# A two-layer decoder step: order of the key groups in layer 1, gate pages by GpSimd, index keys by pairs, outputs turned whole

## The chip, the core and the metric

The kernel runs on one core of a Trainium2 chip. Times are microseconds of that core. TensorE (PE) multiplies and turns tiles and loads its weights on a unit of its own (PEld); VectorE (DVE), ScalarE (ACT) and GpSimd (POOL) work elementwise; SyncE (SP) and, here and there, ScalarE and GpSimd issue the DMA transfers. A transpose is work of PE: it takes the tile and an identity matrix and writes to PSUM, from where another engine copies it.

## What is computed

One inference step of a decoder with two layers: 256 prompt tokens and 8 sample sequences with one new token each behind 2048 cached ones, in float32. Layer 0 is sparse attention with an indexer, layer 1 attention with cumulative forget gates. In each layer four more heads attend to 256 memory tokens, and a mixture of 16 experts follows. The cached keys, values, index keys and gates lie in pages of 128 tokens, found through a page table.

```python
ki_past = pool_ki[page_table].reshape(Bd, P, IDX_DIM)           # layer 0: index keys, 64 wide
sc = indexer_scores(qi, wi, ki_all); _, sel = lax.top_k(sc, 256)
...
k_all = concat([pool_k[page_table], k_new])                     # layer 1: 2048 + 1 keys, 4 heads of 128
lf_all = concat([pool_lf[page_table], logf_new])
c = cumsum(lf_all)                                              # 12 gates for each token
s = q @ k.T * HEAD_DIM ** -0.5 + c_q - c_k
o = softmax(s) @ v
...
mem: o = softmax(qm @ mk.T) @ mv                                # 4 heads, 256 tokens
h = layer_norm(alpha * h + concat([o, o_mem]) @ w_o)
h = layer_norm(alpha * h + hier_moe(h))
```

## The kernel before

**Tiles.** X holds the 264 tokens (256 + 8) turned, as 16 chunks of 128x264. Weights, cached keys and cached values come in units of 2 MB (128x4096) through a ring of six places; `plan` fixes the order of the units and, by its last argument, the place at which some of them must lie. SP issues them in that order and waits for each place to be free. A `slab` is 64 matmuls that multiply two units with X (or with the memory tokens, tile AT) into four PSUM banks, and ScalarE's `slab` copies the four banks out (`slab_copied` counts). Work can be set beside a slab: the function given as `beside` is called with x = 0 to 15 after every fourth matmul.

**Layer 0's index.** `turn_cached` turns the cached index keys (64 wide) for pairs of sequences: for each of four pages and both sequences one matmul with the identity puts 64 rows of the bank. Each is two records in the trace. Eight such steps stand between slab work and the products of the indexer. When the last score is there VectorE selects the top 256 out of 2049 (`MAX8`, line 2112).

**Layer 1's order on PE.** The `else` branch of the program below: the slabs q0, q1, kv1 (values), q2, kv0 (keys), then four times `key_products` (line 982, two sequences each: scores of the new token against 2 x 2048 keys), with the slabs qm, mkv0 (memory keys) and mkv1 (memory values) between them. Before each group VectorE must have turned the four units of keys (line 2209) in their ring places. Gate pages come on SP's queue, 128 of 6 KB (`GATES_AFTER`); VectorE puts them in place (line 2192), `gates_turned` turns their 16 tiles beside slab kv0, and ScalarE copies them. Rows of keys and memory (`late_rows`, `natural`, line 765) are turned in the middle of group 3. `sample_scores` then turns the cached memory keys (16 steps, line 1034) and multiplies (line 1019), and turns the scores (line 1046).

**Attention.** A loop of n = 0 to 21 alternates the prompt's heads (lines 1064 to 1096) with the values of one sequence (line 1114, two units each in layer 1). ScalarE copies the outputs of a sequence (`ov_copy`), and `fold` multiplies them with a constant that picks the rows of its heads; each fold is 2 (layer 0) or 4 matmuls (layer 1, line 1157), and 4 for a pair of sequences in memory (line 1162). In the end ScalarE copies the folded outputs into AT and counts `at_done`, on which the router's weights and the output projection (line 1251) wait.

**Layer norm.** At a layer's end VectorE centres and scales X in quarters of 4 chunks (lines 2384, 2387), ScalarE applies the parameters (line 1881), and the first slab of the next layer follows. `idle_products` (line 1271) are matmuls without use of their result.

## Time and profile before

| | us |
|---|---|
| median of 3 runs | 2137.57 |
| lowest, highest | 2133.9, 2138.18 |
| the profiled execution's own time | 2131.57 |
| its span in the trace | 2129.8 |
| PE busy in the span | 2047.3 |
| VectorE busy | 773.1 |
| ScalarE busy | 387.6 |
| GpSimd busy | 25.6 |

The mean granted clock of PE is 0.989 of full speed. Layer 0's projections and index end near 330 us, its attention at 432, its experts at 1060; layer 1's projections begin at 1071, its attention ends at 1476, and its experts run to the end. A view in order of time has the start of a group of like instructions, the time until its last one ends, the line, result and sources, and how many records there are; idle time before it and what ended it stand in brackets. In a fence, three dots mark rows left out.

### The profile page before, as it was taken

Reading aid. Unit: us, or ns where it says so; the run is one execution under the profiler, and the core shown is the slowest. Engines: PE = TensorE matmul, PEld = TensorE weight load, DVE = VectorE, ACT = ScalarE, POOL = GpSimd, SP = SyncE. Lnnn points to the kernel's source line nnn. Section 1 sums busy time; section 2 is a strip of 40 time slices with the busy share of each in tenths; the row PEclk is TensorE's granted clock in tenths of the full one; section 3 lists DMA queues with packets and bytes.
Section 4 is the critical chain, followed back from the end, with each engine's and each line's share of the span. In section 5 each row is a group of like instructions: output and inputs, shape, how many; then the busy total and the mean of one; then the engine's idle time right before and its main releaser. Section 6 shows DMA issues by size and latency. Waiting matters only on the chain.

```text
span 2129.8 us, 33851 instructions
## 1 busy us (share of the span) xinstructions
PE 2047.3 (96%) x13356; PEld 1291.9 (61%) x13356; DVE 773.1 (36%) x1278; ACT 387.6 (18%) x932; POOL 25.6 (1%) x43
## 2 busy tenths in 40 slices
PE   8999998999999999999989999899999999999998
PEld 7778886888744435353478867566886344343434
DVE  0229998601752221212330433441138312122223
ACT  1220103500421101010221100342024111010122
POOL 0000002100000000000000000000000000000000
PEclk9999999999999999999999999999999999999999
DMA  9834579964279999999944778899631999999994
GB/s 283 247 119 150 177 252 295 312 235 157 80 292 426 422 429 418 428 426 426 392 139 125 285 277 297 319 386 382 232 132 57 423 426 418 427 414 425 418 427 181
DMA packets 210787, 647.43 MB, mean 304 GB/s; under 512 B 55400, under 2 KB 84857, under 8 KB 181089
## 3 DMA queue, kind: packets, MB, share of 16 engines
q1 hardware_dynamic: 194497, 633.99, 77.2%
q10 hardware_dynamic: 14624, 7.48, 1.4%
q0 software_dynamic: 1536, 4.20, 0.6%
q8 instruction: 87, 1.43, 0.3%
q14 instruction: 43, 0.35, 0.1%
HBM read 639.62 MB, written 5.96 MB: 303 GB/s over the span
## 4 chain that ended last, share of the span: by engine, by line
PE 78%; DMA 11%; SPq 6%; issue 2%; DVE 2%; ACT 1%; ACTq 0%; DVEq 0%
PE bank L749 19%; PE bank L1452 15%; PE bank L1251 11%; PE bank L1499 9%; PE bank L1513 6%; DMA ring<-in_w_down 5%; SPq L427 4%; DMA ring<-in_w_up 4%; PE bank L1425 4%; PE bank L982 3%; DMA ring<-in_cache_b_k 1%; PE bank L1335 1%; PE bank L869 1%; SPq L424 1%; PE bank L1222 1%
## 5 line engine op out<-in xcount | busy, mean ns | idle before, releaser
L1452 PE MATMUL bank<-ring,AT 128*64 128x512 f32 x2048 | 457.5, 596 | 12.2 <-DMA ring<-in_w_up 9.0
L749 PE MATMUL bank<-X,ring 128*128 128x264 f32 x1664 | 387.3, 390 | 6.2 <-ACT X L1881 6.2
L749 PEld LDWEIGHTS bank<-X,ring 128*128 128x128 f32 x1664 | 313.1, 191 | 65.0 <-issue 13.3
L1452 PEld LDWEIGHTS bank<-ring,AT 128*64 128x64 f32 x2048 | 144.0, 137 | 286.3 <-issue 278.8
L1625 ACT ACTIVATE arena<-bank 128x512 f32<-128x512 f32 (+9 forms) x307 | 135.5, 479 | 735.2 <-PE bank L749 252.3
L1499 PE MATMUL bank<-ring,arena 128*64 128x512 f32 x1024 | 224.4, 594 | 18.7 <-ACT arena L1625 13.8
L2601 DVE TENSOR_TENSOR X<-bank,X 128x264 f32<-128x264 f32 x256 | 110.7, 432 | 361.8 <-PE bank L1513 359.8
L1251 PE MATMUL bank<-AT,ring 128*128 128x264 f32 x1024 | 232.3, 390 | 0.0
L1251 PEld LDWEIGHTS bank<-AT,ring 128*128 128x128 f32 x1024 | 196.6, 192 | 34.0
L1499 PEld LDWEIGHTS bank<-ring,arena 128*64 128x64 f32 x1024 | 73.2, 137 | 159.5 <-issue 147.6
L2209 DVE STREAM_TRANSPOSE ring<-ring 128x4096 f32<-128x4096 f32 x24 | 106.5, 4442 | 100.8 <-DMA ring<-in_cache_b_k 100.6
L1625 ACT ACTIVATE AT<-bank 128x512 f32<-128x512 f32 (+4 forms) x180 | 84.0, 493 | 321.9 <-PE bank L1425 193.4
L1513 PE MATMUL bank<-arena 128*128 128x264 f32 x512 | 138.8, 402 | 0.0
L1513 PEld LDWEIGHTS bank<-arena 128*128 128x128 f32 x512 | 89.0, 189 | 70.0 <-DVE X L2601 46.7
L749 PE MATMUL bank<-AT,ring 128*128 128x256 f32 x512 | 111.6, 380 | 0.0
L749 PEld LDWEIGHTS bank<-AT,ring 128*128 128x128 f32 x512 | 97.0, 190 | 14.8 <-issue 1.7
L2112 DVE MAX8 arena<-arena 8x8 f32<-8x2049 f32 (+1 forms) x48 | 79.6, 1659 | 42.7 <-ACT arena L1625 41.3
L1425 PE MATMUL bank<-arena 128*128 128x256 bf16 x768 | 89.5, 273 | 0.0
L1425 PEld LDWEIGHTS bank<-arena 128*128 128x128 bf16 x768 | 74.3, 98 | 13.8 <-issue 2.1
L2113 DVE MATCH_REPLACE8 arena<-arena 8x2049 f32<-8x2049 f32 (+1 forms) x48 | 79.1, 1647 | 0.0
L982 PE MATMUL bank<-ring,arena 32*32 32x512 f32 x1536 | 57.9, 641 | 11.0 <-DVE ring L2209 9.7
L2614 DVE TENSOR_TENSOR arena<-bank,arena 128x512 f32<-128x512 f32 x16 | 11.1, 691 | 150.7 <-PE bank L1452 150.7
(361 smaller groups left out, 1344.8 us busy)
## 6 DMA issues: line engine op xcount, KB each, us to landing
ring<-in_w_gate SPq DMA_DIRECT2D x64, 2048.0 KB, 15.3
ring<-in_w_up SPq DMA_DIRECT2D x48, 2048.0 KB, 16.1
ring<-in_w_down SPq DMA_DIRECT2D x48, 2048.0 KB, 13.2
ring<-in_w_o SPq DMA_DIRECT2D x16, 2048.0 KB, 15.7
ring<-in_w_up SPq DMA_DIRECT2D x32, 1024.0 KB, 7.8
ring<-in_w_down SPq DMA_DIRECT2D x32, 1024.0 KB, 16.0
ring<-in_cache_b_k SPq DMA_DIRECT2D x128, 256.0 KB, 5.5
ring<-in_cache_b_v SPq DMA_DIRECT2D x128, 256.0 KB, 8.1
```

Source lines behind the costliest of these rows:

```text
L427: eng.dma_start(dst(g + k), cache[bass.ds(page, 1)].rearrange("a p w -> (a p) w")).then_inc(sem, 16)
L749: mm = pe.matmul(B[at + f][:, 0:n_tok], u[:, c * 512 + f * P:c * 512 + (f + 1) * P], src[8 * half + c][:, 0:n_tok], start=(half == 0 and c ...
L982: mm = pe.matmul(B[bank + r][out, :], a.Qz[kv // 2][rows, q:q + 32], tiles[b][rows, :, kv * P + 32 * d:kv * P + 32 * d + 32], start=(b < 2 ...
L1251: mm = pe.matmul(B[bank0 + f][:, 0:T], u[:, c * 512 + f * P:c * 512 + (f + 1) * P], Ac[8 * half + c], start=(half == 0 and c == 0), stop=( ...
L1425: mm = pe.matmul(B[GATHER_BANKS[q]][:, c * 2 * P:(c + 1) * 2 * P], M.part[t][k][:, at:at + P], M.sel[:, t * 2 * P:(t + 1) * 2 * P], start= ...
L1452: mm = pe.matmul(B[bank][64 * s:64 * s + 64, :], M.xsT[:, at:at + 64], ring[slots[s][0]][:, c * FE:(c + 1) * FE], start=(half == 0 and c = ...
L1499: mm = pe.matmul(B[2 + q][64 * s:64 * s + 64, :], M.hT[:, at:at + 64], ring[slots[s][0]][:, j * D + q * 512:j * D + (q + 1) * 512], start= ...
L1513: pe.matmul(B[2 + c % 4][:, 0:T], M.ys[:, c * P:(c + 1) * P], M.gt[a], start=True, stop=True).then_inc(sm("scattered"), 1)
L1625: return act.activation(out, in_, ACT.Copy, scale=scale)
L2112: link(dve.max(m8, sc))
L2209: dve.transpose(t[:, :], t[:, :]).then_inc(S("keys_made"), 1)
L2601: dve.tensor_tensor(Xc[c], B[2 + c % 4][:, 0:T], Xc[c], ALU.add).then_inc(sm("scatter_added"), 1)
```

## The change

- Index keys of two sequences lie side by side (`index_key`), and one transpose turns a page of both.
- `fold` becomes `turn_out`: the whole output tile is turned, and VectorE's `place_out` adds up the rows that belong together, in the loop from n = 4 on and behind it. `new_values` moves to the second prompt item and gets columns of its own, which VectorE adds at the end; ScalarE's last copies go. `turn_out(x)` waits until x outputs have been placed.
- Layer 1's slabs and key groups stand in another order; the second memory slab comes behind the last key group, the score turns lie beside it, the exp in front of its copies; memory rows are turned behind it and kept in another place. The bank set of the key groups is now 0 in both layers, and ring places follow the order of use.
- GpSimd issues the gate pages, after its memsets.
- The first quarter of the layer norm is scaled by chunks, and five idle products follow the layer norm of layer 0 on PE.

Names below: `consts` holds the identity, `ring` the 2 MB units, `bank` PSUM. PE of layer 1 from the slab in front of key group 1 to the group itself, before (key products are L982, L1003 after; slabs L749, L747 after):

```order
L749 MATMUL bank<-X,ring 128x264 [waits full5_l1,slab_copied]
L749 MATMUL bank<-X,ring 128x264 x31
L749 MATMUL bank<-X,ring 128x264 [waits full2_l1]
L749 MATMUL bank<-X,ring 128x264 x31
L982 MATMUL bank<-ring,arena 32x512 [waits keys_made]
L982 MATMUL bank<-ring,arena 32x512 x127
L992 MATMUL bank<-consts 32x32 [waits natural_copied,slab_copied]
L992 MATMUL bank<-consts 32x32
```

And after:

```order
L747 MATMUL bank<-X,ring 128x264 [waits full5_l1,slab_copied]
L747 MATMUL bank<-X,ring 128x264 x31
L747 MATMUL bank<-X,ring 128x264 [waits full0_l1]
L747 MATMUL bank<-X,ring 128x264 x31
L787 MATMUL bank<-consts,arena 128x128 [waits lf_ready,slab_copied]
L787 MATMUL bank<-consts,arena 128x128 x15
L1003 MATMUL bank<-ring,arena 32x512 [waits keys_made]
L1003 MATMUL bank<-ring,arena 32x512 x127
L1017 MATMUL bank<-consts 32x32 [waits lf_copied,natural_copied,slab_copied]
L1017 MATMUL bank<-consts 32x32
```

Behind the same slab length stand now the 16 gate transposes (L787), and the group waits for the gates' copies only at its end.

PE from the turned rows in the middle of key group 3 (`late_rows`) on, before:

```order
L765 MATMUL bank<-consts,AT 128x128 [waits natural_copied]
L765 MATMUL bank<-consts,AT 128x128 x3
L765 MATMUL bank<-consts,AT 128x128 [waits natural_copied]
L765 MATMUL bank<-consts,AT 128x128 x3
L982 MATMUL bank<-ring,arena 32x512 x64
L992 MATMUL bank<-consts 32x32 [waits natural_copied,slab_copied]
L992 MATMUL bank<-consts 32x32
L1009 MATMUL bank<-consts,AT 128x1 [waits keys_made,natural_copied]
L1034 MATMUL bank<-consts,ring 128x128 [waits full5_l1,q_padded]
L1034 MATMUL bank<-consts,ring 128x128 x7
```

And after, from the start of group 3:

```order
L1003 MATMUL bank<-ring,arena 32x512 [waits keys_made]
L1003 MATMUL bank<-ring,arena 32x512 x63
L801 MATMUL bank<-consts,arena 128x1 [waits keys_made,slab_copied]
L1003 MATMUL bank<-ring,arena 32x512 x64
L1017 MATMUL bank<-consts 32x32 [waits keys_made,natural_copied,slab_copied]
L1017 MATMUL bank<-consts 32x32
L747 MATMUL bank<-AT,ring 128x256 [waits full5_l1,slab_copied]
L747 MATMUL bank<-AT,ring 128x256 x31
L747 MATMUL bank<-AT,ring 128x256 [waits full0_l1]
L747 MATMUL bank<-AT,ring 128x256 x11
L810 MATMUL bank<-consts,arena 128x128 [waits s_norm]
L810 MATMUL bank<-consts,arena 128x128 x3
```

The rows of keys and memory (L765) are gone from the middle of group 3, where only the new key's score stays (L801); a slab with the score turns (L810) stands in front of the memory-key steps.

GpSimd between its memsets at the start of layer 1, before:

```order
L427 DMA ring<-in_cache_a_v 128x256
L661 MEMSET arena 128x64x8 [waits ln_out]
L663 MEMSET arena 128x2048
L666 MEMSET arena 128x2048 [waits lf_copied]
L668 MEMSET AT 128x1024 [waits memory_done]
L204 UNCONDITIONAL_BRANCH
```

And after, the first of 128 pages:

```order
L423 DMA ring<-in_cache_a_v 128x256
L656 MEMSET arena 128x64x8 [waits ln_out]
L658 MEMSET arena 128x2048
L660 MEMSET arena 128x2048
L420 TENSOR_LOAD ptab
L422 ISA
L423 DMA arena<-in_cache_b_lf 128x12
L422 ISA
L423 DMA arena<-in_cache_b_lf 128x12
```

The page transfers stand between the memset of line 660 and the wait for the memory slab.

```diff
--- before.py
+++ after.py
-        u = units("f", [0]) + units("q", range(4)) + units("kv", range(2, 4)) + units("mem", [0])
-        u += units("q", range(4, 6), 1, 0) + units("kv", [0], 1, 5) + units("kv", [1], 1, 2)
-        for x, name in enumerate(("qm", "mkv", "mkv", "mk")):
-            k, n = (2 if x == 2 else 0), (4 if name == "mk" else 1)
-            u += units("k", range(4 * x, 4 * x + 2), 8, 3) + units("k", range(4 * x + 2, 4 * x + 4), 8, 0)
-            u += units(name, [k], n, 5) + units(name, [k + 1], n, 2)
-        u += units("v", range(16), 8, 3) + units("mv", range(2), 4)
+        u = units("f", [0]) + units("q", range(6)) + units("mem", [0]) + units("kv", range(2, 4)) + units("k", range(4), 8)
+        u += units("kv", range(2)) + units("k", range(4, 8), 8) + units("qm", range(2)) + units("k", range(8, 12), 8)
+        u += units("mkv", range(2)) + units("k", range(12, 16), 8) + units("mkv", range(2, 4)) + units("mk", range(2), 4)
+        u += units("v", range(16), 8) + units("mv", range(2), 4)
...
-                    if layer == 1 and (name, k) in GATES_AFTER:
-                        if GATES_AFTER[name, k][0] == 0:
-                            sp.wait_ge(S("ln_out"), 2 * KC)
-                        for b in GATES_AFTER[name, k]:
-                            pages(S("lf_in"), b, 0, PAGES, i["cache_b_lf"][0],
-                                  lambda g: lay[1].LC[:, (g * NB + b) * H:(g * NB + b + 1) * H])
...
-                    pool.wait_ge(S("lf_copied"), 4)
                     pool.memset(a.Qz[1], 0.0).then_inc(S("zeroed"), 1)
+                if layer == 1:
+                    for b in range(NB):
+                        load_pages(pool, vregs, S("lf_in"), b, 0, PAGES, i["cache_b_lf"][0],
+                                   lambda g: a.LC[:, (g * NB + b) * H:(g * NB + b + 1) * H])
...
+            def gates_turned(a):
+
+                pe.wait_ge(S("slab_copied"), cnt["slab"])
+                pe.wait_ge(S("lf_ready"), 3)
+                for j in range(4):
...
+                        mm = pe.transpose(B[other_banks(1) + j][:, pg * P:(pg + 1) * P],
+                                          a.LF[:, (4 * j + pg) * P:(4 * j + pg + 1) * P], ident)
                     mm.then_inc(S("lf_turned"), 1)
...
+            def key_rows(a):
+
+                pe.wait_ge(S("slab_copied"), cnt["slab"])
+                for t in range(3):
+                    natural(a.kT, a.nk, t, other_banks(1))
...
+            def score_turns(layer, a, j):
+
+                bank = key_banks(layer)
+                if j == 0:
+                    pe.wait_ge(S("s_norm"), 2 * layer + 1)
+                if j < 4:
+                    for pg in range(4):
+                        mm = pe.transpose(B[bank + j][:, pg * P:(pg + 1) * P], a.S[:, (4 * j + pg) * P:(4 * j + pg + 1) * P], ident)
...
+                    b = 2 * g
+                    keys, b = (a.IK, b) if b < IK_EARLY else (late[0], b - IK_EARLY)
                     for pg in range(4):
-                        for s in range(2):
-                            b = 2 * g + s
-                            keys, at = (a.IK, b * PAGES * 64) if b < IK_EARLY else (late[0], (b - IK_EARLY) * PAGES * 64)
-                            at += (4 * j + pg) * 64
-                            mm = pe.matmul(B[n % 2][64 * s:64 * s + 64, pg * P:(pg + 1) * P],
-                                           keys[:, at:at + 64], ident, start=True, stop=True)
+                        at = index_key(b, 4 * j + pg)
+                        mm = pe.transpose(B[n % 2][:, pg * P:(pg + 1) * P], keys[:, at:at + P], ident)
...
+                    if group == 1:
+                        pe.wait_ge(S("lf_copied"), 4)
+                    if group == 3:
+                        pe.wait_ge(S("keys_made"), 27)
...
-                def fold(x):
...
+                def turn_out(x):
                     pe.wait_ge(S("ov_copied"), 12 * layer + x + 1)
                     if x == 0:
                         pe.wait_ge(S("sm_turned"), 2 * layer + 2)
-                        new_values()
-                    if x < NB:
-                        for kv in range(a.nk):
-                            at = (x * a.nk + kv) * HALF
-                            mm = pe.matmul(B[bank + 1][:, at:at + HALF], a.ov[x % 2][:, kv * P:(kv + 1) * P],
-                                           cst("fold6")[:, HALF * (x // 2):HALF * (x // 2 + 1)], start=False, stop=(x == NB - 1 and kv == a.nk - 1))
                     else:
-                        for h in range(HM):
-                            at = NB * a.nk * HALF + ((x - NB) * HM + h) * 2 * HM
-                            mm = pe.matmul(B[bank + 1][:, at:at + 2 * HM], a.ov[x % 2][:, h * P:(h + 1) * P],
-                                           cst("fold4")[:, 8 * (x - NB):8 * (x - NB + 1)], start=True, stop=True)
-                            if h == 0 and x in (NB + 1, NB + 3):
-                                leave(mm, layer, "mv", (x - NB) // 2)
+                        pe.wait_ge(S("at_done"), 13 * layer + x)
+                    for g in range(a.nk if x < NB else HM):
+                        mm = pe.transpose(B[bank + 1][:, g * P:(g + 1) * P], a.ov[x % 2][:, g * P:(g + 1) * P], ident)
+                        if g == 0 and x in (NB + 1, NB + 3):
+                            leave(mm, layer, "mv", (x - NB) // 2)
                     mm.then_inc(S("ov_turned"), 1)
...
                     pe.wait_ge(S("lf_rows_copied"), 1)
-                    slab(layer, "kv", 1, Xc, T, 0, lambda x: turn_memory(layer, x))
-                    slab(layer, "q", 2, Xc, T, 4, lambda x: own_rows(layer, a, x, (a.vT,)))
-                    pe.wait_ge(S("natural_copied"), cnt["natural"])
-
-                    def gates_and_blocks(x):
-                        gates_turned(a, x)
+                    slab(layer, "q", 2, Xc, T, 0, lambda x: turn_memory(layer, x))
+                    pe.wait_ge(S("rows_copied"), cnt["rows_turned"])
+
+                    def blocks(x):
                         if x == 6:
                             query_blocks(layer, a)
 
-                    slab(layer, "kv", 0, Xc, T, 0, gates_and_blocks)
-                    key_products(layer, a, 0)
-                    slab(layer, "qm", 0, Xc, T, 0)
+                    def turned_scores(x):
+                        if 10 <= x <= 14:
+                            score_turns(layer, a, x - 10)
+
+                    slab(layer, "kv", 1, Xc, T, 4, blocks)
+                    key_products(layer, a, 0, lambda: value_rows(a))
+                    slab(layer, "kv", 0, Xc, T, 4)
+                    gates_turned(a)
                     key_products(layer, a, 1)
-                    slab(layer, "mkv", 0, Ac, SEQ, 0)
+                    slab(layer, "qm", 0, Xc, T, 4)
+                    key_rows(a)
                     key_products(layer, a, 2)
-                    slab(layer, "mkv", 1, Ac, SEQ, 0)
-                    key_products(layer, a, 3, lambda: late_rows(layer, a))
+                    slab(layer, "mkv", 0, Ac, SEQ, 4)
+                    key_products(layer, a, 3, lambda: new_key(layer, a).then_inc(S("k_scores"), 1))
+                    slab(layer, "mkv", 1, Ac, SEQ, 4, turned_scores)
+                    late_rows(layer, a)
...
                     layer_norm(layer, n_quad)
+                    idle_products(5)
             last_norm(n_quad)
...
                 late = other_banks(layer)
                 slab(layer, "mkv", 0, heads(a.memK, 4, SEQ), SEQ, late)
+                if layer == 1:
+                    score_exp(layer, a)
+                    turned_scores(layer, a)
                 slab(layer, "mkv", 1, heads(a.mvT, 4, SEQ), SEQ, late)
...
+                def place_out(x):
+
+                    dve.wait_ge(S("ov_turned"), 12 * layer + x + 1)
+                    if x < NB:
+                        rows = turned[:, 0:a.W].rearrange("p (k g r) -> p k r g", g=4, r=32)
+                        for kv in range(a.nk):
+                            h = 8 + HALF * (x // 2) + kv * a.G % HALF
+                            made = dve.tensor_reduce(Av[:, kv * a.G:(kv + 1) * a.G, SEQ + x], rows[:, kv, h:h + a.G, :], AX.X, ALU.add)
+                            if kv < a.nk - 1:
+                                link(made)
+                    else:
+                        m = x - NB
+                        for j in range(2):
+                            rows = diagonal(turned, 64 * j + HM * (2 * m + j), 0, P, [(P + 1, HM), (32, 2)])
+                            made = dve.tensor_reduce(Av[:, H:H + HM, SEQ + 2 * m + j], rows, AX.X, ALU.add)
+                            if j == 0:
+                                link(made)
...
+                    if n >= 4 and n % 2 == 0:
+                        place_out(n // 2 - 2)
+                for x in range(len(ITEMS) // 2 - 1, 12):
+                    place_out(x)
+                dve.wait_ge(S("at_done"), 13 * layer + 12)
+                dve.wait_ge(S("p_out"), base + len(ITEMS))
+                for kv in range(a.nk):
+                    new = B[key_banks(layer)][:, SEQ + 48 * kv:SEQ + 48 * (kv + 1)].rearrange("p (b i) -> p i b", i=HALF)
+                    out, h = Av[:, kv * a.G:(kv + 1) * a.G, SEQ:T], kv * a.G % HALF
+                    made = dve.tensor_tensor(out, out, new[:, h:h + a.G, :], ALU.add)
+                    if kv < a.nk - 1:
+                        link(made)
+                made.then_inc(S("at_done"), 1)
...
-                scale(0)
+                for c in range(4):
+                    dve.tensor_tensor(Xc[c], Xc[c], M.rstd, ALU.mult).then_inc(S("ln_normed"), 1)
...
-                    turn_keys(layer, range(4))
+                    turn_keys(layer, range(8))
                     cached_gates(a)
-                    turn_keys(layer, range(4, 16))
+                    turn_keys(layer, range(8, 16))
```

## Rows read from the trace of the kernel before

**Rows 1.** Stretches: PE, PEld, DVE, ACT, POOL busy us (instructions); PE clock; DMA share; GB/s.

```profile
100.00:150.00 50.00, 49.58 (x420) 34.74 (x419) 7.52 (x9) 17.01 (x34) 1.81 (x1) 1.00 0.21 76
...
1350.00:1400.00 50.00, 42.92 (x591) 26.55 (x595) 18.38 (x47) 22.99 (x53) 0.00 (x0) 0.90 0.87 313
...
1400.00:1450.00 50.00, 47.20 (x534) 34.22 (x526) 21.39 (x58) 20.33 (x69) 0.00 (x0) 1.00 1.05 386
```

**Rows 2.** PE in order of time, layer 0 index: start, duration, line, tiles, count.

```profile
110.78 1.97 PE L869 MATMUL bank<-consts,arena 128*64 128x128 f32 x32
...
112.67 2.05 PE L749 MATMUL bank<-X,ring 128*128 128x264 f32 x8
```

**Rows 3.** PE in order of time, layer 1; idle time before and releaser in brackets.

```profile
1228.33 7.65 PE L982 MATMUL bank<-ring,arena 32*32 32x512 f32 x227
...
1269.57 8.69 PE L982 MATMUL bank<-ring,arena 32*32 32x512 f32 x256 [2.75 <-DVE ring L2209]
...
1377.66 1.11 PE L1034 MATMUL bank<-consts,ring 128*128 128x128 f32 x4 [2.99 <-ACT AT L1625]
...
1384.34 1.97 PE L1046 MATMUL bank<-consts,arena 128*128 128x128 f32 x16
...
1386.14 0.27 PE L1048 MATMUL bank<-consts,arena 128*8 128x128 f32 x1
...
1389.44 1.93 PE L1114 MATMUL bank<-ring,arena 128*32 128x256 f32 x32 [2.41 <-ACT arena L1625]
...
1449.36 1.06 PE L1157 MATMUL bank<-consts,arena 128*128 128x6 f32 x8
...
1450.27 1.11 PE L1071 MATMUL bank<-arena 128*128 128x256 f32 x4
```

**Rows 4.** VectorE in order of time, start of the selection in layer 0.

```profile
145.32 2.28 DVE L2112 MAX8 arena<-arena 8x8 f32<-8x2049 f32 x1 [41.28 <-ACT arena L1625]
```

**Rows 5.** PE in order of time, first slab of layer 1.

```profile
1071.24 9.00 PE L749 MATMUL bank<-X,ring 128*128 128x264 f32 x26 [6.18 <-ACT X L1881]
```

**Rows 6.** VectorE in order of time: layer norm, gates.

```profile
1069.20 1.26 DVE L2387 TENSOR_TENSOR X<-X,arena 128x1056 f32<-128x1056 f32 x1
...
1171.93 1.55 DVE L2192 COPY arena<-arena 128x384 f32<-128x384 f32 x4 [41.22 <-DMA arena<-in_cache_b_lf]
```

**Rows 7.** Short stretches with the granted PE clock (the number before the DMA share).

```profile
1068.00:1076.00 8.00, 4.76 (x11) 3.76 (x12) 7.69 (x7) 4.83 (x10) 0.00 (x0) 0.50 1.05 386
...
1310.00:1312.00 2.00, 2.00 (x48) 0.69 (x42) 0.00 (x0) 0.00 (x0) 0.00 (x0) 0.50 1.06 390
...
1366.00:1374.00 8.00, 7.75 (x76) 5.11 (x74) 5.21 (x6) 5.22 (x10) 0.00 (x0) 1.00 0.79 254
...
1378.00:1380.00 2.00, 2.00 (x14) 0.86 (x13) 0.87 (x2) 0.69 (x2) 0.00 (x0) 0.50 1.05 402
```

**Rows 8.** Waits from 1055 to 1480 us: total, times, longest.

```profile
PE bank L982 <- DVE ring L2209: 9.7, 3, 3.5
...
PE bank L1114 <- DMA ring<-in_cache_b_v: 4.0, 6, 1.3
...
PE bank L1136 <- DMA ring<-in_cache_mem_v: 1.7, 2, 1.2
```

**Rows 9.** SyncE in order of time: start, duration, pages issued.

```profile
1080.95 29.33 SPq L427 DMA_DIRECT2D arena<-in_cache_b_lf  x48
...
1238.70 18.71 SPq L427 DMA_DIRECT2D ring<-in_cache_b_k  x32
```

**Rows 10.** ScalarE in order of time: slab copies, memory rows, padding.

```profile
1347.87 1.22 ACT L1625 ACTIVATE AT<-bank 128x256 f32<-128x256 f32 x4 [40.38 <-PE bank L749]
...
1361.38 1.09 ACT L1625 ACTIVATE AT<-bank 128x512 f32<-128x512 f32 x2 [0.88 <-PE bank L765]
...
1364.47 0.26 ACT L1625 ACTIVATE AT<-arena 128x32 f32<-128x32 f32 x1 [0.46 <-ACT arena L1625]
```

**Rows 11.** GpSimd in order of time, four value pages of layer 0.

```profile
346.24 2.31 POOL L427 DMA_DIRECT2D ring<-in_cache_a_v  x4 [6.76 <-issue]
```

159 lines of the change are left out of this document (84 added, 75 removed).

## The prediction, made before the changed kernel ran

> **What bounds the kernel now.** I read the stretches of 50 us first, then the waits inside those that the change touches. In the expert stages TensorE follows the weight loads; the change leaves them alone and they only shift. In the projections and in attention PE itself carries the end: from 100 to 150 us it is busy 49.58 of 50 us, and the DMA engines are at a share of 0.21. From 1350 to 1400 PE loses 7.08 of 50 us at a mean clock of 0.90, and from 1400 to 1450 the DMA engines are at 1.05 with 386 GB/s [rows 1]: there the loads of the cached values set the pace. So PE work saved before 1200 us counts in full, saved between the key groups only as far as the key loads allow, and saved after 1390 us only if the value loads are ahead.
>
> **Index keys by pairs (layer 0).** In each of eight steps 32 records of 128x128 turn a group of cached index keys (16 identity matmuls of two records), and work on the slab goes on 1.89 us after the first of them (110.78 to 112.67 [rows 2]). Afterwards a step has 8 transposes of one record each. Such a record costs 0.11: 16 of them fill 1384.34 to 1386.14 [rows 3]. A step falls from 1.89 to 0.87, 1.0 us saved in each of 8: **-8.0 us**. What is late next? VectorE starts to select the top 256 when the last index score is copied, at 145.32 after 41.28 us of idle time [rows 4]; it and PE's slabs shift by the same amount and the loads have room, so the gain stays. Bound from below: -4, if copies or products pace the steps.
>
> **Outputs turned whole.** A fold of a sequence in layer 1 is 8 records, 0.91 us to the next matmul (1449.36 to 1450.27 [rows 3]); four transposes at 0.11 cost 0.43. Layer 0 has half as many of each and saves 0.22. Of the four memory folds (8 records each) I credit one, 0.54: the last three transposes now each wait until VectorE has placed the output before, two small reductions and two hand-overs, about what the smaller transposes save. In the loop VectorE's reductions lie beside PE work, which covers them as long as VectorE's softmax is not late. Layer 0: 8 x 0.22 + 0.54 - 0.3 for the additions at the end = **-2.0 us**. Layer 1: 8 x 0.52 + 0.54 - 0.25 = **-4.5 us**. Bounds of both together: -1 and -9.
>
> **Layer norm.** Layer 1's first slab waits 6.18 us for the first chunks of X [rows 5]: VectorE scales 1056 columns in 1.26 us (from 1069.20 [rows 6]) before ScalarE may start. By chunks of 264 the first comes about 0.8 us sooner. The clock stood at 0.50 from 1068 to 1076 us, with 4.76 us of PE work in it [rows 7]; the added idle products keep PE busy in part of the wait. No row shows a kept clock here: bounds 0 and half of 4.76, 2.4; I take 0.7, nearer to nothing, because five short products cover only the start of the gap. **-1.5 us.**
>
> **Layer 1's order.** A slab and a wait for VectorE's turning of the keys stand between two key groups: 9.7 us in three waits [rows 8], the first 2.75 (1269.57 [rows 3]). This is a fixed cycle: SP issues the next keys as soon as group 0 has left its slots (1238.70 [rows 9]), and group 1 starts 30.9 us later, whatever PE does meanwhile. The order leaves the cycle and moves work into it: 16 gate transposes (1.8 us at 0.11) go in front of group 1, the 12 key-row transposes (1.3) in front of group 2. Both were paid outside it. The waits for the slab's copies that they add (four by ScalarE, 1.22 us [rows 10]) lie under the same cover. Behind group 2's wait the clock is at 0.50 (1310 to 1312 us [rows 7]); with a shorter wait this goes, 1.5. 1.8 + 1.3 + 1.5 = **-4.6 us**; bounds 0 (cycle longer by as much) and -6. The memory slab that goes behind group 3 keeps its length.
>
> **Exp and score turns beside a slab.** In the memory-key steps ScalarE's exp stands in its queue in front of the copies: PE waits 2.99 us at 1377.66 [rows 3] and goes on at 0.50 of the clock from 1378 to 1380 [rows 7], 1.3. The first values wait 2.41 us at 1389.44 [rows 3] for the copies of turned scores. The turns stay PE work, in another place. Less 1.2 for a hand-over of the exp to the second memory slab's turns: **-5.5 us**; bounds -3 and -6.7.
>
> **A new wait behind the last slab.** Today the memory rows' copies run beside group 3's second half. Afterwards the slab's copies (1.22), the first four transposes (0.43) and ScalarE's copies of the rows with their stores and the padding of the queries (1361.38 to 1364.73, 3.35 us [rows 10]) stand alone: 5.3 with hand-overs, of which 1.75 are transposes that PE does in any case. 3.6, and 0.8 for a lower clock behind: **+4.4 us**, bounds +2 and +6. Queued behind this wait on PE are all memory-key steps, and attention behind them.
>
> **Values sooner.** PE waits 4.0 us for cached values and 1.7 for memory values in attention [rows 8]. Their loads can start when group 3 has left the ring. Attention starts 20 us after that today, and 27.9 (slab) + 5.3 + 16.4 (memory-key steps) = 49.6 us after it then (the 16.4 are today's 20 less the waits and turns that leave these steps). A sequence is 4.19 MB, 10.9 us at 386 GB/s [rows 1]; PE alone needs 9.5 for it. Counted from group 3's end, with six ring places of 2 MB, the last memory values land at 121.5 us and PE is through at 128.5: both waits go, **-5.7 us**; bound 0. The output weights may start 0.5 late: **+0.5**.
>
> **Gate pages from GpSimd.** VectorE waits for them until 1171.93 [rows 6]. SP issues 48 in 29.33 us, 0.61 each [rows 9]. GpSimd issues four value pages in 2.31 us, 0.58 each, and then stands 6.76 us, in which its code waits for the pages before it goes on [rows 11]. Without that wait I take 0.61 a page: from 1083 us 128 pages end at 1161, landed by 1168. PE will want key group 0 one slab and the gate turns sooner than 1228.33 [rows 3], at 1195 or somewhat later; ahead of it VectorE needs 1.55 for the gates [rows 6] and four times 4.4 for the keys. So gates landed by 1176 cost **0**, and each microsecond beyond stalls group 0. SP, relieved of them, has its key pages earlier, but their slots decide.
>
> **Sum**, on the clock of the old trace: -8.0 - 2.0 - 4.5 - 1.5 - 4.6 - 5.5 + 4.4 - 5.7 + 0.5 = -26.9. The profiled execution took 2131.57 us, 1.8 more than its span and 6 less than the median of the runs shown; from its span the sum gives 2102.9. The runs to come are better compared with the median: 2137.57 - 26.9 = **2110.7 us**.
>
> **The rivals.** *B, part is given back.* The wait behind the memory slab at its upper bound (+1.6), hand-overs of the last outputs (+2), value loads that still pace the end (+4), a key cycle longer by the gate turns (+3), the half clock as now (+2.5): 13.1 of the 26.9 are gone, **2123.8 us**. For it: 386 GB/s at a share of 1.05 is all that the loads give. Chance 0.20.
>
> *C, GpSimd's issue becomes the bound, slower than before.* VectorE places the gates ahead of every key transposition, and no row shows more than four issues in a row. With the gap counted in, (2.31 + 6.76) / 4 = 2.3 us a page, the gates land near 1380 and the time is near 2315, the far bound. At 1.1 us a page they land at 1228, 52 us past 1176: **2163 us**. It equals the old time at about 0.9 us a page. Against it: the gaps stand just where the code waits. Chance 0.08. The Trainium skill ("DMA: Bandwidth & Descriptors", Anatomy of one DMA) fits a transfer issued there by about 2.0 us plus its bytes over 436 GB/s; taken as a price per issue this would make an estimated 256 us for the pages and put the time near 2280. The same section puts most of that into completion, and with the 0.58 us between two issues the trace agrees with the latter.
>
> *D, transposes let the clock fall.* The eight index steps with their slab work and products, 31 us, would take about 28 us longer at half clock: **2138 us**, no change. Against it: from 1366 to 1374 us half of PE's work is transposes, at a clock of 1.00 [rows 7]. Chance 0.04. The Trainium skill ("TensorE: Matmul & The Clock Gate", Part 4: PE-mode transpose) says that a transpose does not count as PE activity in the same way; the rows at 1.00 do not bear that out in a mix like this one.
>
> *E, more.* The layer norm's clock in full (1.7), no clock loss and no hand-over behind the memory slab (2.4), a shorter key cycle (1.4), folds at their bound (2.5), the steps' copies freer (2.7): another 10.7, **2100 us**. Chance 0.08.
>
> **How the numbers follow.** The forecast has 0.60, with a range of its own of 2102 to 2118. The range takes in B's far side and most of E: **2099 to 2130**; C, D and edges of B and E, under 2 in 10, stay out. A measurement of this kernel tells 0.2% (4.3 us) from no change. Faster: the forecast, nearly all of B, and E, 0.87. Same: D and the tail of B, 0.05. Slower: C, 0.08.
>
> **What would show it.** Index steps of 0.9 instead of 1.9 us; the granted clock at 1.00 from 100 to 150 us, or else D. Key groups 31 us apart with the waits in front of the first two nearly gone. No wait for ScalarE in the memory-key steps, one of 3 to 5 us in front of them, none for values. VectorE's placing of the gates before 1176; past 1190 it is C. The sum is most likely wrong where two savings share one cover: the value loads and the turned outputs.

## The result, and the profile after

The changed kernel takes 2112.09 us (median of 4 runs, 2108.60 to 2116.12) against 2135.74 us of the kernel before on the same chips (4 runs, 2129.87 to 2138.18). The ratio is 0.9897 with a 95% interval of 0.9878 to 0.9915: 22 us, or 18 to 26. Run again beside the experiments it was 0.9877 (0.9862 to 0.9891). The forecast was 2110.7 us, 26.9 us less than its base, inside 2099 to 2130. The profiled execution after has a span of 2106.9 us, 22.9 less than that of before.

The page of the changed kernel: PE is busy for 18 us less, GpSimd for 68 us more, which is the 128 page issues.

```profile
span 2106.9 us, 33418 instructions
...
PE 2029.5 (96%) x13094; PEld 1267.8 (60%) x13094; DVE 784.2 (37%) x1352; ACT 385.1 (18%) x924; POOL 93.6 (4%) x171
...
q0 software_dynamic: 5632, 4.99, 1.1%
```

I set marks at places that both kernels have, and subtract the start of the stage from its end. Minus is a gain:

| Stage | before | after | difference | forecast |
|---|---|---|---|---|
| start to the selection (layer 0) | 145.32 | 136.43 | -8.9 | -8.0 |
| to the router's turns of layer 0 | 286.37 | 283.34 | -3.0 | -2.0 |
| experts of layer 0, to the sums | 632.21 | 633.10 | +0.9 | 0 |
| sums to the first scores of attention, layer 1 | 322.35 | 315.35 | -7.0 | -4.8 |
| attention of layer 1, to the router's turns | 90.08 | 83.77 | -6.3 | -12.6 |
| output projection | 102.92 | 101.32 | -1.6 | +0.5 |
| experts of layer 1, to the end | 550.55 | 553.59 | +3.0 | 0 |
| sum | 2129.80 | 2106.90 | -22.9 | -26.9 |

(-4.8 is -1.5 for the norm, -4.6 for the order, -3.1 of the -5.5 for exp and turns, and +4.4 for the new wait; the other -2.4 belong to attention's first wait, with -4.5 and -5.7. These are one trace each; how far a row can be trusted stands in the experiments, under the same kernel again.)

The index in layer 0, PE in order of time. A transpose is one record here, and the eight of a step fill 0.92 us up to the next slab matmul, against 1.89 in [rows 2]. The 8 slab records behind them last 1.95 instead of 2.05 us. The granted clock of the stretch is 1.00, and VectorE's selection starts at 136.43 (before: [rows 4]):

```profile
108.31 1.09 PE L893 MATMUL bank<-consts,arena 128*128 128x128 f32 x8
...
109.23 1.95 PE L747 MATMUL bank<-X,ring 128*128 128x264 f32 x8
...
136.43 2.28 DVE L2134 MAX8 arena<-arena 8x8 f32<-8x2049 f32 x1 [32.55 <-ACT arena L1647]
...
100.00:150.00 50.00, 49.58 (x267) 35.08 (x266) 16.14 (x15) 15.96 (x34) 1.81 (x1) 1.00 0.35 132
```

The first slab of layer 1 waits 0.99 us behind the idle products (L1286) where it waited 6.18 [rows 5], and the granted clock is 1.00 from 1056 to 1068 us where it was 0.50 around that wait [rows 7]:

```profile
1053.86 4.46 PE L1286 MATMUL bank<-consts 128*128 128x512 f32 x10
...
1059.31 16.04 PE L747 MATMUL bank<-X,ring 128*128 128x264 f32 x71 [0.99 <-ACT X L1900]
...
1056.00:1060.00 4.00, 3.01 (x9) 1.42 (x8) 3.93 (x7) 2.54 (x5) 0.00 (x0) 1.00 1.05 387
...
1060.00:1068.00 8.00, 8.00 (x37) 6.83 (x37) 6.84 (x6) 5.68 (x12) 0.00 (x0) 1.00 0.79 290
```

The four key groups on PE, to be read beside [rows 3, 8]. There is a wait in front of group 0 that was not there before (2.35 us), the waits in front of groups 1 and 2 are now for ScalarE's copies of the slab (1.33 each), and that of group 3 stays:

```profile
1184.29 4.45 PE L1003 MATMUL bank<-ring,arena 32*32 32x512 f32 x128 [2.35 <-DVE ring L2231]
...
1224.76 1.97 PE L787 MATMUL bank<-consts,arena 128*128 128x128 f32 x16 [1.33 <-ACT arena L1647]
...
1226.66 9.78 PE L1003 MATMUL bank<-ring,arena 32*32 32x512 f32 x256
...
1266.60 1.53 PE L763 MATMUL bank<-consts,arena 128*128 128x128 f32 x12 [1.33 <-ACT arena L1647]
...
1268.06 5.52 PE L1003 MATMUL bank<-ring,arena 32*32 32x512 f32 x160
...
1308.84 6.06 PE L1003 MATMUL bank<-ring,arena 32*32 32x512 f32 x128 [2.70 <-DVE ring L2231]
```

What group 0 waits for shows on VectorE and GpSimd. GpSimd needs 4.71 us for eight pages and 0.66 between eights; the gates are placed at 1165.04, and VectorE turns all four key units behind them without a pause, so each of them had landed when its turn came:

```profile
1165.04 1.54 DVE L2214 COPY arena<-arena 128x384 f32<-128x384 f32 x4 [49.41 <-DMA arena<-in_cache_b_lf]
...
1166.72 17.42 DVE L2231 STREAM_TRANSPOSE ring<-ring 128x4096 f32<-128x4096 f32 x4
...
1073.31 11.05 POOL L423 DMA_DIRECT2D arena<-in_cache_b_lf  x21
...
1151.02 4.14 POOL L423 DMA_DIRECT2D arena<-in_cache_b_lf  x7 [2.95 <-issue]
...
1155.82 4.71 POOL L423 DMA_DIRECT2D arena<-in_cache_b_lf  x8 [0.67 <-issue]
```

Behind the last slab PE waits 1.30 and 2.16 us, the new wait, and the memory-key steps then run without ScalarE's exp in their queue (2.99 us in [rows 3]). At the end of attention the waits for values are still there, 2.5 and 1.6 us (4.0 and 1.7 in [rows 8]). SP issues the value pages from 1325.38 us on (before: 1366.78), but the DMA engines stand at a share of 0.79 from 1350 to 1370, and from 1345 to 1375 SP waits 8.1 us for ring places that the memory-key steps (L1042) have not yet left. PE in order of time, its waits from 1370 to 1460 us, and two stretches:

```profile
1350.77 1.09 PE L763 MATMUL bank<-consts,arena 128*128 128x128 f32 x8 [1.30 <-ACT AT L1647]
...
1354.89 1.06 PE L1057 MATMUL bank<-consts,ring 128*128 128x128 f32 x8 [2.16 <-ACT arena L1647]
...
1369.03 1.93 PE L1136 MATMUL bank<-ring,arena 128*32 128x256 f32 x32
...
1433.48 1.93 PE L1136 MATMUL bank<-ring,arena 128*32 128x256 f32 x32 [1.00 <-DMA ring<-in_cache_b_v]
...
1438.97 1.07 PE L1158 MATMUL bank<-ring,arena 128*32 128x512 f32 x8 [1.64 <-DMA ring<-in_cache_mem_v]
...
1451.99 0.68 PE L1291 MATMUL bank<-consts,ring 80*128 80x80 f32 x4 [1.36 <-issue]
...
PE bank L1136 <- DMA ring<-in_cache_b_v: 2.5, 3, 1.0
...
PE bank L1158 <- DMA ring<-in_cache_mem_v: 1.6, 1, 1.6
...
1350.00:1370.00 20.00, 16.65 (x170) 11.08 (x174) 1.54 (x4) 11.83 (x24) 0.54 (x1) 1.00 0.79 265
...
1370.00:1390.00 20.00, 19.95 (x253) 13.24 (x246) 11.03 (x41) 8.84 (x36) 0.00 (x0) 1.00 1.02 358
```

### The profile page after: what moved, and what is told of

The parts are those of the page before. It is cut to its first block, busy times and chain, and to the rows that moved or that the text cites. A ratio compares the mean times of both kernels' runs of the same rounds, so it can differ in the third digit from the quotient of the medians.

```text
span 2106.9 us, 33418 instructions
## 1 busy us (share of the span) xinstructions
PE 2029.5 (96%) x13094; PEld 1267.8 (60%) x13094; DVE 784.2 (37%) x1352; ACT 385.1 (18%) x924; POOL 93.6 (4%) x171
## 4 chain that ended last, share of the span: by engine, by line
PE 46%; issue 38%; DMA 9%; SPq 3%; DVE 1%; POOLq 1%; POOL 1%; ACT 1%; ACTq 0%; DVEq 0%
PE bank L747 16%; PE bank L1467 7%; PE bank L1266 5%; DMA ring<-in_w_down 4%; PE bank L1514 4%; PE bank L1528 3%; PE bank L1003 2%; SPq L423 2%; DMA ring<-in_w_up 2%; PE bank L1440 2%; DMA ring<-in_cache_a_v 1%; DVE ring L2231 1%; POOLq L420 1%; POOL arena L423 1%; DMA ring<-in_cache_mem_v 1%
## 5 line engine op out<-in xcount | busy, mean ns | idle before, releaser
L747 PE MATMUL bank<-X,ring 128*128 128x264 f32 x1664 | 382.6, 388 | 1.0 <-ACT X L1900 1.0
L747 PEld LDWEIGHTS bank<-X,ring 128*128 128x128 f32 x1664 | 311.6, 190 | 58.3 <-issue 7.2
L1647 ACT ACTIVATE AT<-bank 128x512 f32<-128x512 f32 (+1 forms) x170 | 81.8, 504 | 277.0 <-PE bank L1440 193.7
L747 PE MATMUL bank<-AT,ring 128*128 128x256 f32 x512 | 112.4, 380 | 0.0
L747 PEld LDWEIGHTS bank<-AT,ring 128*128 128x128 f32 x512 | 96.6, 190 | 14.7 <-issue 1.7
L423 POOL DMA_DIRECT2D arena<-in_cache_b_lf x128 | 68.3, 535 | 19.0 <-issue 13.4
L2682 DVE TENSOR_TENSOR arena<-bank,arena 128x512 f32<-128x512 f32 x16 | 11.1, 692 | 150.7 <-PE bank L1467 150.7
## 6 DMA issues: line engine op xcount, KB each, us to landing
ring<-in_w_gate SPq DMA_DIRECT2D x64, 2048.0 KB, 16.2
ring<-in_w_down SPq DMA_DIRECT2D x48, 2048.0 KB, 13.3
```

The lines of the kernel that those rows point to most:

```text
L423: eng.dma_start(dst(g + k), cache[bass.ds(page, 1)].rearrange("a p w -> (a p) w")).then_inc(sem, 16)
L747: mm = pe.matmul(B[at + f][:, 0:n_tok], u[:, c * 512 + f * P:c * 512 + (f + 1) * P], src[8 * half + c][:, 0:n_tok], start=(half == 0 and c ...
L1647: return act.activation(out, in_, ACT.Copy, scale=scale)
```

## The experiments

Each kernel was traced once, and the marks of its stages were taken as above. "The change" is the changed kernel. Where a time is given, runs of the kernel before on the same chip stand beside it.

### The same kernel again, and how much a stage scatters

No edit.

> The changed kernel once more, beside the three that follow, so that their marks in the trace have a neighbour from the same chip. If the differences of 3 us in the experts' stages between the two first traces (index end, attention end, router, end) are a matter of the single execution, the marks up to the output projection repeat within 0.3 us and the expert stages scatter by some us; if the change itself makes the second expert stage 3 us longer, it is 553.6 us again and 550.6 in the kernel before.

Measured: 2108.32 us, ratio 0.9877 (0.9862 to 0.9891). Its trace puts the selection at 136.61 and the sums at 1052.69, like the first one. Sums to attention is 318.83 (first trace 315.35), attention 84.31 (83.77), experts of layer 1 552.54 (553.59). Against the expectation the marks do not repeat within 0.3 us: the same kernel scatters by 3.5 us between sums and attention, 1.56 in key group 0, 0.8 in group 2 and 1.5 in the memory-key steps. In group 0 the granted clock was 0.57 from 1184 to 1188 us (1.00 in the first trace). In the memory-key steps, 14.84 us here and 13.33 in the first trace, it was below 1.00 too:

```profile
1356.00:1360.00 4.00, 3.07 (x20) 2.33 (x24) 0.00 (x0) 2.21 (x5) 0.00 (x0) 0.79 0.92 313
...
1360.00:1364.00 4.00, 4.00 (x36) 2.54 (x32) 0.00 (x0) 1.98 (x5) 0.00 (x0) 0.78 0.77 293
...
1364.00:1368.00 4.00, 4.00 (x44) 2.51 (x37) 0.00 (x0) 2.69 (x6) 0.00 (x0) 1.00 0.45 137
```

Over the fourteen traces the experts of layer 0 take 631.3 to 636.1 us and those of layer 1 550.6 to 555.7, changed or not; in the kernel before and its three variants the latter are 550.55, 552.36, 551.39 and 552.16. The trace of before was at the low end. The +3.0 us of the table is this scatter for the most part, not a cost of the change. A difference of a few us in a total therefore needs its stage.

The other rows scatter as well. Sums to attention takes 322.35, 319.26 and 315.06 us in the kernel before and the two variants with its code there (pairs alone, outputs alone), and 315.35, 318.83 and 320.50 in three traces with the code of the change there (the last is that of the half-loaded values). The -7.0 of the table is thus not shown. The output projection takes 101.3 to 104.2 us, changed or not, so its -1.6 says nothing. Attention of layer 1 is clear of its scatter: 89.1 to 90.9 us with the old folds in the old order, 83.1 to 84.3 in the nine traces with the new order and all loads.

### Index keys by pairs alone

In the kernel before, only the pages of two sequences side by side and one transpose for both:

```diff
-                        for s in range(2):
...
-                            mm = pe.matmul(B[n % 2][64 * s:64 * s + 64, pg * P:(pg + 1) * P],
-                                           keys[:, at:at + 64], ident, start=True, stop=True)
+                        at = index_key(b, 4 * j + pg)
+                        mm = pe.transpose(B[n % 2][:, pg * P:(pg + 1) * P], keys[:, at:at + P], ident)
```

> The kernel before with the index keys by pairs alone. Theory: each of eight steps shortens by 1.0 us, VectorE's selection starts at about 137 us instead of 145.3, attention of layer 0 ends 8 to 9 us sooner (before: 431.7), total -8 to -9 us. Rival: the selection on VectorE is not the only chain behind the index and part of the gain waits for key loads: attention ends less than 5 us sooner.

Measured: 2122.79 us, ratio 0.9941 (0.9924 to 0.9959), that is 12.6 us less (8.8 to 16.2). Selection at 135.53 us, 9.8 sooner, the router's turns at 420.10, 11.6 sooner. The theory holds and was a little low: beside the eight steps the slab matmuls right behind each got 0.1 us shorter per eight records. The shorter way from the selection to the router's turns (284.57 instead of 286.37 us) is within what this stretch scatters; nothing was given back up to the experts.

### Outputs turned whole alone

In the kernel before, `fold` replaced by `turn_out` and `place_out`, as in the diff of the change; all else as before.

> The kernel before with the outputs turned whole alone. Theory of the prediction: -2.0 us in layer 0, -4.5 us in layer 1. Rival: in layer 1 the value loads pace the end of attention; what the folds save turns into waits for values (5.7 us before become 8 to 9), the memory part at the end gets longer by the hand-overs, and layer 1 gains 0 to 1 us; total -3 us.

Measured: 2126.48 us, ratio 0.9963 (0.9948 to 0.9978). Layer 0, selection to router: 284.23 against 286.37 us, -2.1, as forecast. But the two other kernels with the old folds have 284.57 and 285.83 there, so one trace does not settle it. Layer 1, attention: 91.66 against 90.08 (89.06 and 90.91 in the two others), so at least not shorter. PE's waits for values and memory values in it rose from 5.7 to 10.6 us:

```profile
PE bank L1121 <- DMA ring<-in_cache_b_v: 7.9, 9, 1.4
...
PE bank L1143 <- DMA ring<-in_cache_mem_v: 2.7, 2, 1.6
```

From the end of key group 3 to the router's turns it is 110.4 us; the kernel before has 110.2. The rival holds in the attention of layer 1: there the folds were not on the path, the value loads were. Its total of -3 does not. The total is still 7.9 us lower (4.7 to 11.1), of which the trace has 7.3 between the sums and attention, where this kernel's code is that of before: the three intervals from a group's end to the next group are 28.9, 28.9 and 31.4 us instead of 31.4, 31.4 and 31.3. The key units landed more evenly in this trace: VectorE waits 0.9 to 1.2 us between the units of groups 1 and 2, where it waited up to 1.98 before, and PE waits 0.22 and 1.11 us in front of these groups instead of 2.75 and 3.54. So the interval of the old order follows the landing of the keys and is not fixed at 31 us. Why they landed sooner, and whether that repeats, one trace cannot tell.

### Half of the value pages left out

The changed kernel loads 4 of 8 pages in each unit of cached values of layer 1; the rest of a unit is what lay in the ring, so the sample tokens' output of layer 1 is not the reference's.

```diff
-        u += units("v", range(16), 8) + units("mv", range(2), 4)
+        u += units("v", range(16), 4) + units("mv", range(2), 4)
...
-                        if layer == 0:
-                            per -= POOL_PAGES
+                        per -= POOL_PAGES
```

> The changed kernel with half the cached value pages of layer 1 left out (the multiplications run on what lies in the ring). Theory: PE waits 4.1 us for values and memory values; without the loads these go and attention of layer 1 shortens by 4 to 5 us (83.8 from the first scores to the router's turns). Rival: other hand-overs (softmax, output copies) are just behind, and it shortens by 1 us or less.

Measured: PE has no wait for the DMA engines in attention at all (all its waits from 1370 to 1480 us stand below), and attention takes 78.2 us (1376.93 to 1455.18) instead of 83.8. The total, one run, was 2113.10 us: not below the change, as sums to attention (320.50 us) and output projection (104.16) were slow in this trace. From the end of group 3 to the router's turns it is 127.9 us; the change has 132.2 and 134.3 in its two traces. The prediction had 128.5, that is, the time without load waits. In the seven other kernels with the new order it is 131.5 to 133.3, and in the four kernels with the old order 110.2 to 111.0. The new order puts a slab of 27.9 us into this interval and, with all that was saved in it, pays 22 for it.

```profile
PE bank L1290 <- issue: 1.4, 1, 1.4
...
PE bank L1177 <- DVE AT L2309: 1.1, 2, 0.6
...
PE bank L1041 <- ACT AT L1646: 0.2, 1, 0.2
```

### Gates: three ways to place them

First, the kernel before with only the gate pages moved to GpSimd (ahead of its wait for `lf_copied`).

> The kernel before with the gate pages issued by GpSimd alone. Theory: PE did not wait for the gates in the kernel before, SP's key pages wait for their ring places, so the total stays (within 1 us); the page issues end near 1171 us and VectorE places the gates near 1176, 4 us later than before. Rival: a later placing of the gates pushes the turning of the keys, or SP, free of 85 us of issues, brings the keys sooner: a shift of 2 us or more of group 0 (1228.3) one way or the other.

Measured: 2134.97 us (10 runs, one of them at 8274.28 and outside the ratio), ratio 1.0004 (0.9984 to 1.0023). VectorE places the gates at 1176.17 instead of 1171.93, group 0 starts at 1227.48 (1228.33). The theory holds: alone, the move shows neither a cost nor a gain, to within 4 us.

Second, the change with the gate pages back on SP, which issues them as in the kernel before, behind the units named here.

```diff
+GATES_AFTER = {("q", 4): (0, 1, 2), ("mem", 0): (3, 4), ("kv", 2): (5, 6, 7)}
...
-                    for b in range(NB):
-                        load_pages(pool, vregs, S("lf_in"), b, 0, PAGES, i["cache_b_lf"][0],
```

> The changed kernel with the gate pages back on SP's queue, behind the third query slab, the memory tokens and the first value weights. Theory: SP now has 78 us of page issues on its queue in front of key units that group 0 wants one slab sooner than before; the four key units land later by 10 us or more and group 0 starts 5 us or more later than 1184.3, so that the issue by GpSimd is what lets the new order work. Rival: the queue has room, group 0 starts within 1 us of 1184.3, and GpSimd's issue is worth nothing.

Measured: 2118.37 us, ratio 0.9913 (0.9884 to 0.9941). SP now reaches the first key unit at 1155.71 (change: 1120.90). Group 0 starts 136.6 us after the sums instead of 131.4 and waits 7.53 us for the turned keys. The gates are placed early, at 1155.81; what is late are the keys. By these traces the move to GpSimd is worth 5 us in the new order; in the old one no gain shows. SP and then VectorE in order of time, and group 0 on PE:

```profile
1155.71 20.35 SPq L424 DMA_DIRECT2D ring<-in_cache_b_k  x32
...
1155.81 1.55 DVE L2217 COPY arena<-arena 128x384 f32<-128x384 f32 x4 [39.65 <-DMA arena<-in_cache_b_lf]
...
1185.40 4.45 DVE L2234 STREAM_TRANSPOSE ring<-ring 128x4096 f32<-128x4096 f32 x1 [0.98 <-DMA ring<-in_cache_b_k]
...
1189.99 3.06 PE L1006 MATMUL bank<-ring,arena 32*32 32x512 f32 x38 [7.53 <-DVE ring L2234]
```

Third, the change with ten more clears of a 128x2048 tile on GpSimd ahead of the pages.

```diff
+                    for k in range(10):
+                        pool.memset(a.Qz[1], 0.0).then_inc(S("slow"), 1)
+                        pool.wait_ge(S("slow"), k + 1)
                     pool.memset(a.Qz[1], 0.0).then_inc(S("zeroed"), 1)
```

> GpSimd clears its second query tile ten times more before it issues the gate pages: the pages start some 19 us later (ten times 1.80 us and the hand-overs). Theory: from the threshold on each microsecond of GpSimd stalls group 0, so the wait in front of group 0 grows from 2.3 to about 21 us and the time rises by 18 to 19 us. Rival: the pages run faster when nothing else loads beside them, or later waits shrink, and the time rises by 12 us or less.

Measured: 2134.84 us, ratio to the kernel before 1.0006 (0.9992 to 1.0020): all the gain is gone. The clears took 18.60 us; from the sums the gates are placed 23.8 us later than in the change and group 0 starts 23.8 us later, one for one. The wait in front of it is 26.19 us, more than the 21 expected. Of the 5 us beyond the clears 3 are a pause of 5.94 us in front of GpSimd's last 15 pages, where the change has 2.95. So the mechanism of the prediction's rival C is real, with the price it was given (each microsecond of later gates costs one); its condition, a dearer page, was not met.

```profile
1069.01 18.60 POOL L661 MEMSET arena<- 128x2048 f32 x10
...
1172.34 4.14 POOL L423 DMA_DIRECT2D arena<-in_cache_b_lf  x7 [5.94 <-issue]
...
1186.32 1.54 DVE L2217 COPY arena<-arena 128x384 f32<-128x384 f32 x4 [73.24 <-DMA arena<-in_cache_b_lf]
...
1205.57 3.22 PE L1006 MATMUL bank<-ring,arena 32*32 32x512 f32 x48 [26.19 <-DVE ring L2234]
```

### Keys turned before the gates are placed

```diff
-                    place_gates(a)
-                    turn_keys(layer, range(8))
+                    turn_keys(layer, range(4))
+                    place_gates(a)
+                    turn_keys(layer, range(4, 8))
```

> VectorE turns the four key units of group 0 before it places the gates, nothing else is changed. Theory: group 0 waits 2.35 us in the changed kernel only because the gates, which land at 1165 us, stand ahead of keys that landed earlier; then the wait in front of group 0 is 0, group 0 starts 2.4 us sooner, the whole cycle behind it shifts, -2.4 us in all. Rival: the keys of group 0 had themselves just landed (after 1160 us), and less than 0.5 us of the wait goes; total no change.

Measured: 2109.83 us, ratio 0.9888 (0.9870 to 0.9906). In the trace the wait in front of group 0 is gone and it starts 129.0 us after the sums instead of 131.4: the 2.4 us of the theory. VectorE has the last key unit of the group turned at 1176.3, 9.4 us before PE starts on it without a wait (1185.65). The totals (2108.32 for the change beside it) don't show it; 2.4 us lie within the scatter of these runs.

```profile
1171.82 4.45 DVE L2231 STREAM_TRANSPOSE ring<-ring 128x4096 f32<-128x4096 f32 x1 [1.20 <-DMA ring<-in_cache_b_k]
...
1176.18 1.50 DVE L2214 COPY arena<-arena 128x384 f32<-128x384 f32 x4
...
1185.65 2.95 PE L1003 MATMUL bank<-ring,arena 32*32 32x512 f32 x79
```

### Without the part on the layer norm, and without the idle products alone

```diff
-                    idle_products(5)
...
-                for c in range(4):
-                    dve.tensor_tensor(Xc[c], Xc[c], M.rstd, ALU.mult).then_inc(S("ln_normed"), 1)
+                scale(0)
```

> The changed kernel without the part on the layer norm (first quarter scaled whole, no idle products). Theory: the first slab of layer 1 starts 0.8 to 0.9 us later after the sums, and the clock is at half for some 10 us around it as in the kernel before, which costs about 3 us more: key group 0 comes 3 to 4 us later. Rival (the prediction's size): 1.5 us later in all.

> The changed kernel without the five idle products only. Theory: scaling by chunks keeps its 0.9 us, the half clock comes back: 3 us against the changed kernel. Rival: the shorter wait alone keeps the clock, 0 us.

Measured, as times from the sums to the point at which PE wants group 0 (its start less the wait for VectorE in front of it): the change 129.1, without the idle products 130.7, without both 132.7 us. So the whole part moves PE's work 3.6 us ahead, 1.6 of it by the idle products. Without them PE stands 5.28 us, and the clock is at 0.50 from 1056 to 1060 us and at 0.83 from 1060 to 1068. Group 0 itself starts at 131.4, 132.4 and 133.0 us: as the gates hold it in the change, only 1.6 of the 3.6 us came through. Between the two theories on record it is the first on PE and the second on the path. The totals, one run each, were 2117.67 us without both and 2116.62 without the idle products; one run cannot tell them apart. The two stretches are those without the idle products, the last line is group 0 without both:

```profile
1056.00:1060.00 4.00, 0.51 (x1) 0.50 (x2) 3.93 (x7) 2.55 (x5) 0.00 (x0) 0.50 1.05 386
...
1060.00:1068.00 8.00, 8.00 (x31) 6.57 (x30) 7.01 (x6) 5.68 (x12) 0.00 (x0) 0.83 0.79 291
...
1186.45 4.45 PE L1003 MATMUL bank<-ring,arena 32*32 32x512 f32 x128 [0.31 <-DVE ring L2230]
```

### Memory-key rows earlier, and both edits

The rows of the memory keys are turned in front of group 3 and stored from another place.

```diff
+                    late_rows(layer, a, (a.memK,))
                     key_products(layer, a, 3, lambda: new_key(layer, a).then_inc(S("k_scores"), 1))
                     slab(layer, "mkv", 1, Ac, SEQ, 4, turned_scores)
-                    late_rows(layer, a)
+                    late_rows(layer, a, (a.mvT,))
```

> The rows of the memory keys are turned in front of key group 3 and stored from another place; only those of the memory values stay behind the last slab. Theory: 8 transposes and their copies move into the wait in front of group 3 (2.70 us), the wait of 2.16 us in front of the memory-key steps falls to about 0.6, and attention starts 2.4 us sooner; the end of attention follows in full, -2.4 us. Rival: the value loads pace the end of attention, they start at the end of group 3, which does not move, so the waits for values and memory values (2.48 and 1.64 us) grow by what was gained and attention ends at the same distance from group 3: 0 us.

Measured: 2108.30 us, ratio 0.9880 (0.9866 to 0.9895), as the change beside it. The wait in front of the memory-key steps fell from 2.16 to 1.50 us, not to 0.6, and that in front of group 3 from 2.70 to 0.96. From group 3 to the memory-key steps it is 33.6 instead of 35.1 us, but group 3 starts 31.2 us after group 2's end instead of 30.3 to 30.5. From group 3's end to the router's turns it is 131.8 (change: 132.2, 134.3). That fits the rival, loads that pace the end, but doesn't prove it: the remaining difference is smaller than the scatter.

With both edits together:

> Both edits together. Theory of the two independent waits: -4.8 us against the changed kernel beside it. Rival (loads pace the end of attention): only the part in front of group 0 counts, -2.4 us.

Measured: 2106.71 us (6 runs, 2100.15 to 2112.31), ratio 0.9879 (0.9861 to 0.9897). The trace has group 0 at 129.0 us from the sums. 2106.71 is the lowest median of all, by 1.6 us under the change beside it, and not to be told from it by these runs.

## Why the prediction was right, point by point

The total was right, by 1.4 us, and part of that is luck. The trace gained 22.9 us where the sum had 26.9, and the medians differ by 23.7. The base helped: the forecast was put on a median of 2137.57 us, and the kernel before now had 2135.74. Among the terms, misses in both directions made up for each other in part.

- **Index keys, -8.0**: right, a little low (-8.9 in the change, -9.8 alone). What was missing is the slab work behind each turn, which got shorter too. It stayed, as argued: the router's turns came 11.6 us sooner with this part alone.
- **Outputs turned whole, layer 0, -2.0**: -2.1 alone, which fits but lies within the scatter of that stretch.
- **Outputs turned whole, layer 1, -4.5, and values sooner, -5.7**: the step that failed, as mechanism. The text itself named it as the weakest place, "two savings share one cover". (A slip beside it: a fold of 0.91 us less 0.43 is 0.48, not the 0.52 of the sum, 0.3 us in all.) Before the change the values paced the end of attention (alone, the turned outputs gave nothing there and the waits grew from 5.7 to 10.6 us). After it they still do, with 4.1 us of waits. Attention gave 6.3 us instead of 12.6. The assumption "both waits go" is refuted by the trace, and the half-loaded values show what it was worth: without load waits attention is 5.5 us shorter (78.2), and the way from group 3 on is 127.9 us against 132.2 and 134.3. The head start is bounded: the DMA engines are at a share of only 0.79 from 1350 to 1370 us, while SP waits for ring places and PE has hardly begun to use values.
- **Layer norm, -1.5**: mis-sized. On PE it is -3.6. The clock has a larger part in it than assumed: with the idle products and the shorter wait it is at 1.00 from 1056 to 1068 us.
- **Gate pages, 0**: wrong by 2 us. A page costs 0.67 us ((4.71 + 0.66) / 8), not 0.61, and there is a pause of 2.95 us near the end. These used up the margin of the forecast: the gates came at 1165 us on a clock 11 us ahead of the old one, which is just the threshold of 1176. And the norm part made PE want group 0 some 2 us earlier than the threshold assumed. The two errors belong together: 3.6 us gained by the norm part and 2.0 lost to the gates (2.35 us of wait in the change, 0.31 without the norm part) give the 1.6 that the norm term had by chance. Each microsecond past the threshold costs one, as said (the late pages).
- **Layer 1's order, -4.6**: not shown. No run has the order alone, and sums to attention scatters by more than this term. The fixed cycle behind it holds only as a coincidence. Groups start 31.9, 31.5 and 30.5 us after the one before ended, before 31.4, 31.4 and 31.3. But in front of groups 1 and 2 this is now PE's own chain (slab 28.75, copies 1.33, turns 1.9 or 1.5); the waits for VectorE are gone, not shortened. And with the old order the interval was 28.9 us twice in one kernel (outputs alone). The granted clock behind group 2's wait did rise (1.00 from 1268 to 1272 us), but the 1.5 us for it don't show in the group's length: 10.07 us before, 10.10 and 10.92 after, with a pause of 1.18 us in the middle.
- **New wait, +4.4**: 3.5 us (1.30 and 2.16), and a lower clock behind it (0.79 and 0.78) came in the repeated trace but not in the first. In size right.
- **Exp and turns, -5.5**: the 2.99 and the 2.41 us waits are gone, and the clock is at 1.00 from 1350 to 1370 us. The 1.2 us put down for a hand-over did not come: PE has no wait inside the second memory slab. Right, and a little low.
- **Rivals**: of B (part given back, 2123.8) one mechanism came, value loads that still pace the end, priced at 4 and worth 4 to 6 us. Hand-overs of the last outputs show as 1.1 us of waits for VectorE; the longer key cycle and the longer wait behind the memory slab did not come. D (clock) is refuted: 1.00 from 100 to 150 us. The Trainium skill ("TensorE: Matmul & The Clock Gate", Part 4: PE-mode transpose) says that a transpose does not count as PE-busy for the clock in the same way; this is a second row that doesn't bear it out where transposes stand beside slab work. C did not come, as pages cost 0.67 us in a row of 128.

What each part gives by the totals stays partly open: the two parts measured alone come to 12.6 and 7.9 us of the 22 to 26, with intervals of 8.8 to 16.2 and 4.7 to 11.1, and 7.3 of the 7.9 appeared in a stage that the edit does not touch.

## What to carry to other kernels

Before two savings in one stage are added, ask whether a load stream paces its end: take the time from the point where the stream may start to the end of the stage, in both orders, and compare it with the bytes. A forecast that hits the total can still be wrong in its terms; marks at places that both kernels share, and one part done alone, tell that at the price of a few runs. Trace the same kernel twice before a stage's difference is read: here one stage moved by 3.5 us with no edit. Where an engine serves two waits in a fixed order (gates ahead of keys on VectorE), put first what has landed first.

## What was not expected of the hardware

- Replacing the identity matmuls of two records by half as many transposes of one made the slab matmuls behind them shorter too: eight records 1.95 instead of 2.05 us. Pieces of the same slab that do not follow a transpose still take 2.05.
- GpSimd's page issues hold their rate over 128 pages (535 ns each, 0.60 us apart within eight) but pause in front of the same page, the 114th, in all ten traces in which GpSimd issues them: 2.95 us in the change, 2.86 in its repeat, 2.91 in the old order, 5.94 with late pages. In the kernel with the gates alone, in the old order, SP issues its first key page only after the pause (1167.28 against 1162.31 us), so the key pages are not its cause. What it waits for stays open.
- In one and the same kernel a wait of 2.16 us before the memory-key steps was followed by a granted clock of 1.00 in one trace (13.3 us for the steps) and of 0.79 and 0.78 over 8 us in another (14.8 us).
